# Weight sums of the up projections as a four-deep pipeline, and 16 instead of 8 blocks of layer 0 in seven products

## The chip, the cores and the metric

The kernel runs on one core of a Trainium2 chip. Its time is the device time of one launch, in microseconds (us). The core has TensorE (PE in the profile; PEld is its weight load), VectorE (DVE), ScalarE (ACT), GpSimd (POOL) and SyncE (SP). SP and POOL issue the large DMAs here: SP's go through the queue that the page calls q1 (hardware), POOL's through q0 (software). Both feed the same 16 DMA engines.

## The reference, cut to what matters

Two transformer layers over 512 tokens of width 1024, in fp32. Each is an attention and a feed-forward part:

```python
def conv_ffn(h, w_up, conv_w, conv_b, w_down):
    a, gate = jnp.split(h @ w_up, 2, axis=-1)          # w_up: 1024 x 5632
    a = lax.conv_general_dilated(a, ...) + conv_b      # 3 taps along the sequence
    return (jax.nn.silu(a) * gate) @ w_down            # w_down: 2816 x 1024

for i in range(2):
    x = x + attention_i(rms_norm(x, attn_norm[i]))     # layer 0: sliding window with sinks; layer 1: differential
    x = x + conv_ffn(rms_norm(x, ffn_norm[i]), ffn_w_up[i], ...)
return rms_norm(x, final_norm)
```

## The kernel before

**Products.** Every fp32 operand is cut into a high part (ACT writes it, rounded to fp32r) and a low part (DVE: the value less the high part). `hi_lo` (L764) makes one product of three matmuls (L766 to L768). The order on PE is written out by hand: attention of layer 0 (4 units), its output projection, 22 blocks of the up projection, 22 of the down projection, then the same for layer 1 with 8 units.

**The up projection, classical.** A block is 128 columns of `a` and the 128 matching columns of `gate`. `up_pair` (L1247) does two blocks. A block is 2 sides x 8 chunks of the contraction x 3 matmuls = 48 matmuls of 512 columns. Its weights are 1 MB, loaded by SP in two DMAs (L598).

**The up projection, in seven products.** `seven_products` (L1284) treats the block as a 2x2 block product (halves of the contraction, halves of the tokens, `a` against `gate`) and takes Strassen-Winograd's seven half-size products: 7 x 4 chunks x 3 = 84 matmuls of 256 columns. The left operands are weights and four sums of weights, S1 to S4. Per block SP loads 1.75 MB: in `load_seven` (L618) 0.25 MB (L629) and 0.5 MB (L630) of plain weights and 0.75 MB of sums (L631), in `load_fourth` (L605) 0.25 MB of S4 (L615). `PLAIN = (14, 6)` says how many blocks of each layer are classical: 14 of 22 in layer 0, 6 of 22 in layer 1. All load through the two halves of `raw`; a load waits until DVE has taken the low part of the block two before it, and ACT takes a block's high part once PE is done with the block two before it.

**The sums.** They lie in two DRAM tensors, `w_sums0` and `w_sums1`. POOL makes them with DMAs alone, in rounds (`weight_sums`, L727), each for 128 rows and 1024 columns: four copies DRAM to DRAM (L736 to L739), wait, two accumulating DMAs (L741, L742), wait, one (L744), wait, one (L746), wait. A DMA moves 0.5 MB. Layer 0 has one chunk of columns (`CHUNKS = (1, 2)`), so 4 rounds; layer 1 two chunks, so 8. SP waits (L625) for a chunk's sums ahead of the first load from it. `BEFORE_ROUND` holds POOL back: layer 0's round 0 until the load of attention unit 3 has landed, its round 3 until that of up block 3, and layer 1's round 2 until that of layer 1's unit 2. Rounds run without a stop otherwise.

## Time and profile before

| | us |
|---|---|
| median of 3 runs | 1111.3 (1111.16 to 1111.36) |
| the profiled execution | 1111.62 |
| its span in the profile | 1109.8 |
| rounds of sums of layer 0 begin at | 40.4, 73.2, 105.6, 178.0 |
| rounds of layer 1 begin at | 208.2, 250.0, 527.6, 569.7, 611.3, 652.7, 692.1, 731.3 |
| POOL's last DMA of layer 0 / of layer 1 is issued at | 202.7 / 765.3 |
| issue to landing of the second DMA of the up pairs issued at 194, 215, 226, 237, 259, 269 | 6.0, 8.5, 9.6, 7.0, 6.3, 6.5 |
| packets and MB, SP's queue / POOL's | 182430, 120.32 / 13824, 50.34 |
| SP issues the first load of a product block, layer 0 / layer 1 | 291.1 / 796.9 |

1.8 us of the profiled execution lie outside its span. "Idle before" in a timeline is the time that an engine stood still before an instruction, with what ended it. In a POOL row of a DMA the duration is that of issuing it only; when it landed is seen from the next row's wait. DMA share is the mean busy share of the 16 DMA engines in a stretch. PE's matmuls overlap one another, so the distance between two starts is what one costs, not its duration.

### The profile page before, as it was taken

How to read it: one execution, taken by the hardware profiler on the slowest of the kernel's cores; microseconds unless marked ns; L12 is line 12 of the kernel's file. 1: busy time of each engine (PE TensorE's matmuls, PEld its weight loads, DVE VectorE, ACT ScalarE, POOL GpSimd, SP SyncE). 2: the span in 40 equal slices, each digit the busy share in tenths (PEclk: the TensorE clock that was granted, in tenths of full speed). 3: DMA queues.
4: the chain of work that ended last, by engine and by line, in shares of the span. 5: the costliest groups of instructions: out<-in, count | busy, mean ns of one | idle time of the engine just before them, and what ended most of it. 6: DMA issues, size and time to landing. Idle time of an engine off the chain costs nothing.

```text
span 1109.8 us, 17573 instructions
## 1 busy us (share of the span) xinstructions
PE 1098.8 (99%) x6408; PEld 984.2 (89%) x6408; DVE 807.0 (73%) x1374; ACT 550.2 (50%) x1064; POOL 69.0 (6%) x116
## 2 busy tenths in 40 slices
PE   9999999999999999999999999999999999999997
PEld 8999888888899988888999999788889999998886
DVE  6888866557998863337788788857998888876335
ACT  6878653222255433335666666645344554443334
POOL 1111101111000000000111111110000000000000
PEclk9999999999999999999999999999999999999999
DMA  6767546999556422226888777777446656422322
GB/s 201 213 184 182 103 153 186 220 169 233 152 153 180 147 76 94 94 94 190 199 161 173 172 171 136 130 191 171 140 127 199 199 171 177 143 95 98 98 102 99
DMA packets 196330, 171.35 MB, mean 154 GB/s; under 512 B 14425, under 2 KB 176438, under 8 KB 196278
## 3 DMA queue, kind: packets, MB, share of 16 engines
q1 hardware_dynamic: 182430, 120.32, 35.9%
q0 software_dynamic: 13824, 50.34, 23.6%
q8 instruction: 31, 0.51, 0.2%
q14 instruction: 21, 0.17, 0.1%
q10 hardware_dynamic: 24, 0.01, 0.0%
HBM read 168.55 MB, written 52.43 MB: 199 GB/s over the span
## 4 chain that ended last, share of the span: by engine, by line
PE 91%; DVE 5%; ACT 2%; issue 1%; DMA 1%; SPq 0%; DVEq 0%; ACTq 0%
PE ps L766 23%; PE ps L767 23%; PE ps L768 23%; PE ps L842 15%; PE ps L883 2%; PE ps L1065 2%; PE ps L1084 1%; PE ps L944 1%; DMA raw<-in_a_w_in 1%; ACT w_hi L1429 1%; DVE w_lo L2012 0%; DVE h_lo L2044 0%; DVE xT L2376 0%; DVE x_tok L2731 0%; DVE ssacc L2037 0%
## 5 line engine op out<-in xcount | busy, mean ns | idle before, releaser
L768 PE MATMUL ps<-h_hi,w_hi 128*128 128x256 f32 (+1 forms) x704 | 233.2, 331 | 0.0
L767 PE MATMUL ps<-h_lo,w_hi 128*128 128x256 f32 (+1 forms) x704 | 233.2, 331 | 0.0
L766 PE MATMUL ps<-h_hi,w_lo 128*128 128x256 f32 (+1 forms) x704 | 233.2, 331 | 0.0
L1429 ACT ACTIVATE w_hi<-raw 128x512 fp32r<-128x512 f32 (+2 forms) x180 | 146.0, 842 | 86.0 <-PE ps L768 83.1
L2012 DVE TENSOR_TENSOR w_lo<-raw,w_hi 128x512 fp32r<-128x512 f32 (+2 forms) x180 | 167.9, 957 | 11.2 <-ACT w_hi L1429 11.0
L766 PEld LDWEIGHTS ps<-h_hi,w_lo 128*128 128x128 f32 x704 | 133.8, 190 | 12.6
L768 PEld LDWEIGHTS ps<-h_hi,w_hi 128*128 128x128 f32 x704 | 133.8, 190 | 12.5
L767 PEld LDWEIGHTS ps<-h_lo,w_hi 128*128 128x128 f32 x704 | 133.8, 190 | 12.4
L842 PE MATMUL ps<-w_hi,h_lo 128*128 128x384 f32 x368 | 126.1, 343 | 0.6 <-DVE w_lo L2012 0.4
L842 PE MATMUL ps<-w_hi,h_hi 128*128 128x384 f32 x368 | 125.7, 342 | 0.0
L842 PE MATMUL ps<-w_lo,h_hi 128*128 128x384 f32 x368 | 125.5, 341 | 0.0
L2405 DVE TENSOR_TENSOR u_lo<-u_all,u_hi 128x512 fp32r<-128x512 f32 x44 | 30.4, 691 | 123.4 <-ACT u_hi L1721 123.4
L1721 ACT ACTIVATE u_hi<-u_all 128x512 fp32r (+1 forms) x44 | 27.6, 631 | 142.2 <-PE ps L768 142.1
L766 PE MATMUL ps<-u_hi,w_lo 128*128 128x512 f32 (+1 forms) x272 | 95.9, 353 | 0.2
L768 PE MATMUL ps<-u_hi,w_hi 128*128 128x512 f32 (+1 forms) x272 | 95.6, 352 | 0.0
L767 PE MATMUL ps<-u_lo,w_hi 128*128 128x512 f32 (+1 forms) x272 | 95.6, 352 | 0.0
L2468 DVE TENSOR_TENSOR w_lo<-raw,w_hi 128x1536 fp32r<-128x1536 f32 x48 | 83.7, 1751 | 0.0
L842 PEld LDWEIGHTS ps<-w_hi,h_lo 128*128 128x128 f32 x368 | 69.2, 188 | 5.2 <-DVE v_lo L2067 2.9
L842 PEld LDWEIGHTS ps<-w_hi,h_hi 128*128 128x128 f32 x368 | 69.2, 188 | 0.8
L842 PEld LDWEIGHTS ps<-w_lo,h_hi 128*128 128x128 f32 x368 | 69.2, 188 | 0.3
L766 PE MATMUL ps<-w_hi,u_lo 128*128 128x512 f32 x176 | 68.6, 390 | 0.0
L768 PE MATMUL ps<-w_hi,u_hi 128*128 128x512 f32 x176 | 68.5, 389 | 0.0
(254 smaller groups left out, 2229.8 us busy)
## 6 DMA issues: line engine op xcount, KB each, us to landing
w_sums<-in_ffn_w_up POOLq DMA_DIRECT2D x72, 512.0 KB, 7.7
raw<-in_ffn_w_up SPq DMA_DIRECT2D x64, 512.0 KB, 5.2
raw<-in_ffn_w_down SPq DMA_DIRECT2D x44, 512.0 KB, 3.3
raw<-w_sums SPq DMA_DIRECT2D x24, 768.0 KB, 7.0
w_sums<-w_sums POOLq DMA_DIRECT2D x24, 512.0 KB, 7.3
raw<-in_b_w_in SPq DMA_DIRECT2D x24, 512.0 KB, 5.8
raw<-in_ffn_w_up SPq DMA_DIRECT2D x24, 256.0 KB, 3.0
s_raw<-w_sums SPq DMA_DIRECT2D x24, 256.0 KB, 3.7
```

The lines of the kernel that those rows point to most:

```text
L766: pe.matmul(out_, a_lo, b_hi, start=start, stop=False)
L767: pe.matmul(out_, a_hi, b_lo, start=False, stop=False)
L768: return pe.matmul(out_, a_hi, b_hi, start=False, stop=stop)
L842: ins = pe.matmul(ps[:, pj(u, t), 0:UW], a[:, kc, tok], b[:, kc, :], start=(kc == kc0 and m == 0), stop=(kc == kc1 and m == 2))
L883: ins = pe.transpose(ps[:, bank, c * P:(c + 1) * P], i, ident[:, :])
L944: ins = pe.matmul(ps[:, bank, 0:2 * P], head_queries(a)[:, g, :, :], keys_of(b, t, j), start=(m == 0), stop=(m == 2))
L1065: ins = pe.matmul(ps[:, s_bank(t) + e, 0:n], a[rows, 0, q], b[rows, 1, 0:n], start=(m == 0), stop=(m == 2))
L1429: act.activation(w_hi[:, s, at], raw[:, s, at], ACT.Copy).then_inc(hi_done, 1)
L1721: act.activation(u_hi[:, s, :], u_all[:, bass.ds(f, 1), :], ACT.Copy).then_inc(uhi_done, 1)
L2012: dve.tensor_tensor(w_lo[:, s, at], raw[:, s, at], w_hi[:, s, at].bitcast(F32), ALU.subtract).then_inc(lo_done, 1)
L2405: dve.tensor_tensor(u_lo[:, s, :], u_all[:, bass.ds(f, 1), :].rearrange("p a b -> p (a b)"), u_hi[:, s, :].bitcast(F32), ALU.subtract).the ...
L2468: dve.tensor_tensor(w_lo[:, s, at], raw[:, s, at], w_hi[:, s, at].bitcast(F32), ALU.subtract)\
```

## The change

`PLAIN` becomes `(6, 6)` and `CHUNKS` `(2, 2)`: layer 0 has 16 blocks in seven products too, and 8 rounds of sums in two chunks. Rounds are no longer done one after the other: step n issues the two additions of round n-1, the third addition of round n-2, the fourth of round n-3 and the four copies of round n, and then waits for all of them; a layer takes its rounds and three more steps. POOL is held back only at the beginning of each layer's sums: in layer 0 until the load of unit 2 (of attention) has landed, in layer 1 until that of its unit 2. `sums_in` is the new count for which SP waits: steps 0 to 6 for a layer's first chunk, all 11 for its second.

```diff
-PLAIN = (14, 6)
-CHUNKS = (1, 2)
+PLAIN = (6, 6)
+CHUNKS = (2, 2)
...
-BEFORE_ROUND = {(0, 0): ("attnA", 3), (0, 3): ("up0", 3), (1, 2): ("attnB", 2)}
+BEFORE_STEP = {(0, 0): ("attnA", 2), (1, 0): ("attnB", 2)}
...
             c = (f - PLAIN[l]) * P // SUM_COLS[l]
-            return ((CHUNKS[0] if l else 0) + c + 1) * HALF_D // P * DMAS * 16
+            steps = range(4 * c + 4 + 3)
+            n = 4 * CHUNKS[l]
+            before = 4 * CHUNKS[0] * DMAS if l else 0
+            return 16 * (before + sum(4 * (k < n) + 2 * (1 <= k <= n) + (2 <= k <= n + 1) + (3 <= k) for k in steps))
...
+                begun = 0
+                if n - 1 in range(len(rounds)):
+                    begun += add(block(n - 1, 0), part(n - 1, 0, F))
+                    begun += add(block(n - 1, 1), part(n - 1, 0, F))
+                if n - 2 in range(len(rounds)):
+                    begun += add(block(n - 2, 2), block(n - 2, 0))
+                if n - 3 in range(len(rounds)):
+                    begun += add(block(n - 3, 3), block(n - 3, 2))
+                if n in range(len(rounds)):
+                    begun += copy(block(n, 0), part(n, 1, F))
+                    begun += copy(block(n, 1), part(n, 0, 0))
+                    begun += copy(block(n, 2), part(n, 0, 0))
+                    begun += copy(block(n, 3), part(n, 1, 0))
+                return begun
...
-                for n, (c, rows) in enumerate(rounds):
-                    if (l, n) in BEFORE_ROUND:
-                        after_load(*BEFORE_ROUND[l, n])
-                    weight_sums(l, rows, c, done)
-                    done += DMAS * 16
+                for n in range(len(rounds) + 3):
+                    if (l, n) in BEFORE_STEP:
+                        after_load(*BEFORE_STEP[l, n])
+                    done += sum_step(l, n, rounds) * 16
+                    pool.wait_ge(sum_landed, done)
```

POOL's program before, one round of layer 0 and the beginning of the next. `w_sums0` is the DRAM tensor of layer 0's sums; L736 to L739 are copies, L741 to L746 additions:

```order
L736 DMA w_sums0<-in_ffn_w_up 128x1024 [waits sum_landed]
L737 DMA w_sums0<-in_ffn_w_up 128x1024
L738 DMA w_sums0<-in_ffn_w_up 128x1024
L739 DMA w_sums0<-in_ffn_w_up 128x1024
L741 DMA w_sums0<-in_ffn_w_up 128x1024 [waits sum_landed]
L742 DMA w_sums0<-in_ffn_w_up 128x1024
L744 DMA w_sums0<-w_sums0 128x1024 [waits sum_landed]
L746 DMA w_sums0<-w_sums0 128x1024 [waits sum_landed]
L736 DMA w_sums0<-in_ffn_w_up 128x1024 [waits sum_landed]
```

The same engine now, layer 0 from its step 3 to its step 5 (L745 is an addition, L750 a copy):

```order
L745 DMA w_sums0<-in_ffn_w_up 128x1024 [waits sum_landed]
L745 DMA w_sums0<-in_ffn_w_up 128x1024
L745 DMA w_sums0<-w_sums0 128x1024 x2
L750 DMA w_sums0<-in_ffn_w_up 128x1024 x4
L745 DMA w_sums0<-in_ffn_w_up 128x1024 [waits sum_landed]
L745 DMA w_sums0<-in_ffn_w_up 128x1024
L745 DMA w_sums0<-w_sums0 128x1024 x2
L750 DMA w_sums0<-in_ffn_w_up 128x1024 x4
L745 DMA w_sums0<-in_ffn_w_up 128x1024 [waits sum_landed]
```

Eight DMAs stood behind four waits; now eight stand behind one.

ACT's program before, in the feed-forward part of layer 0: a loop over two classical blocks (high parts of two blocks' weights, and two SiLUs), which runs four times, then the code that leads over to the product blocks. Before:

```order
L1806 UNCONDITIONAL_BRANCH
L1806 ISA
L1427 ISA
L1429 ACTIVATE w_hi<-raw 128x2048
L1725 ACTIVATE gated<-conv 128x512
L550 REGISTER_ALU
L1427 REGISTER_ALU
L1429 ACTIVATE w_hi<-raw 128x2048
L1725 ACTIVATE gated<-conv 128x512
L1806 REGISTER_ALU
L1806 COMPARE_AND_BRANCH
L1429 ACTIVATE w_hi<-raw 128x2048
```

Now the code that leads over stands at the head of the part:

```order
L1445 ACTIVATE w_hi<-raw 128x2048
L1741 ACTIVATE gated<-conv 128x512
L1445 ACTIVATE w_hi<-raw 128x2048
L1741 ACTIVATE gated<-conv 128x512
L1754 ACTIVATE u_hi<-u_all 128x1024
L1445 ACTIVATE w_hi<-raw 128x2048
L1741 ACTIVATE gated<-conv 128x512
L1754 ACTIVATE b21_ops<-u_all 128x1024
L1754 ACTIVATE b22_ops<-u_all 128x1024
L1445 ACTIVATE w_hi<-raw 128x2048
L1741 ACTIVATE gated<-conv 128x512
L1774 ACTIVATE w_hi<-raw 128x1536
```

The loop is gone (with 6 classical blocks it would run no time, as in layer 1), so the operands of the seven products are made from block 0 on instead of from block 8 on.

## Rows read from the trace of the kernel before

**Rows 1.** The page, part 1: busy us, share of the span, instructions, by engine.

```profile
PE 1098.8 (99%) x6408; PEld 984.2 (89%) x6408; DVE 807.0 (73%) x1374; ACT 550.2 (50%) x1064; POOL 69.0 (6%) x116
```

**Rows 2.** Timeline of PE at phase borders: start us, us, engine, line, operation.

```profile
152.69 0.39 PE L766 MATMUL ps<-ot_hi,w_lo 128*128 128x512 f32 x1
...
163.57 0.39 PE L766 MATMUL ps<-h_hi,w_lo 128*128 128x512 f32 x1
...
316.42 0.28 PE L766 MATMUL ps<-u_hi,w_lo 128*128 128x256 f32 x1
...
397.24 0.40 PE L766 MATMUL ps<-u_hi,w_lo 128*128 128x512 f32 x1
...
754.72 0.39 PE L766 MATMUL ps<-h_hi,w_lo 128*128 128x512 f32 x1
...
820.53 0.28 PE L766 MATMUL ps<-u_hi,w_lo 128*128 128x256 f32 x1
...
982.19 0.27 PE L1342 MATMUL ps<-ident,xT 128*128 128x128 f32 x1
```

**Rows 3.** Windows, product blocks: stretch, length, PE PEld DVE ACT POOL busy, clock, DMA, GB/s.

```profile
340.00:360.00 20.00, 20.00 (x169) 20.00 (x168) 16.86 (x23) 9.82 (x13) 0.00 (x0) 1.00 0.64 180
```

**Rows 4.** Timeline of POOL, two rounds of sums: last bracket is idle time before.

```profile
105.56 0.54 POOL L736 DMA_DIRECT2D w_sums<-in_ffn_w_up  x1 [4.56 <-DMA w_sums<-w_sums]
...
114.27 0.84 POOL L741 DMA_DIRECT2D w_sums<-in_ffn_w_up  x1 [6.61 <-DMA w_sums<-in_ffn_w_up]
...
122.64 0.81 POOL L744 DMA_DIRECT2D w_sums<-w_sums  x1 [6.67 <-DMA w_sums<-in_ffn_w_up]
...
128.18 0.80 POOL L746 DMA_DIRECT2D w_sums<-w_sums  x1 [4.73 <-DMA w_sums<-w_sums]
...
208.23 0.54 POOL L736 DMA_DIRECT2D w_sums<-in_ffn_w_up  x1 [4.76 <-DMA w_sums<-w_sums]
...
221.44 0.84 POOL L741 DMA_DIRECT2D w_sums<-in_ffn_w_up  x1 [11.06 <-DMA w_sums<-in_ffn_w_up]
...
233.03 0.81 POOL L744 DMA_DIRECT2D w_sums<-w_sums  x1 [9.89 <-DMA w_sums<-in_ffn_w_up]
...
250.02 0.54 POOL L736 DMA_DIRECT2D w_sums<-in_ffn_w_up  x1 [8.05 <-DMA w_sums<-w_sums]
```

**Rows 5.** One line's DMAs in a stretch (durations ns of the issue), then issue to landing.

```profile
L571 SPq DMA_DIRECT2D raw<-in_a_w_in x1: 5177/5177/5177, 24.4 to 24.4; - x1
DMA to landing us min/median/max: 9.4/9.4/9.4
...
L592 SPq DMA_DIRECT2D raw<-in_a_w_out x1: 368/368/368, 142.6 to 142.6; - x1
DMA to landing us min/median/max: 4.7/4.7/4.7
...
L598 SPq DMA_DIRECT2D raw<-in_ffn_w_up x2: 373/408/442, 776.6 to 777.2; - x2
DMA to landing us min/median/max: 3.8/4.2/4.7
...
L598 SPq DMA_DIRECT2D raw<-in_ffn_w_up x2: 373/842/1312, 225.9 to 226.4; - x2
DMA to landing us min/median/max: 8.4/9.0/9.6
...
L631 SPq DMA_DIRECT2D raw<-w_sums x1: 436/436/436, 356.6 to 356.6; - x1
DMA to landing us min/median/max: 7.1/7.1/7.1
```

**Rows 6.** Timelines of ACT, DVE and PE around block 20 of layer 0.

```profile
367.74 1.47 ACT L1758 ACTIVATE w_hi<-raw 128x1536 fp32r<-128x1536 f32 x1
...
373.60 1.75 DVE L2468 TENSOR_TENSOR w_lo<-raw,w_hi 128x1536 fp32r<-128x1536 f32 x1
...
377.08 0.28 PE L766 MATMUL ps<-u_hi,w_lo 128*128 128x256 f32 x1
```

More of the change, by code:

```diff
@@ L725, in _ @@
                     pool.memset(tensor[(1 - e) * HD:(2 - e) * HD, e, :].bitcast(F32), 0.0).then_inc(kz_done, 1)
-            def weight_sums(l, rows, c, done):
-                wv, sums = ffn_w_up[l], w_sums[l]
-                a, gate = PLAIN[l] * P + c, PLAIN[l] * P + c + F
-                def part(half, at):
-                    return wv[half * HALF_D + rows:half * HALF_D + rows + P, at:at + SUM_COLS[l]]
-                s1, s3, s2, s4 = (sums[q * HALF_D + rows:q * HALF_D + rows + P, c:c + SUM_COLS[l]] for q in range(4))
-                pool.dma_start(s1, part(1, gate)).then_inc(sum_landed, 16)
-                pool.dma_start(s3, part(0, a)).then_inc(sum_landed, 16)
-                pool.dma_start(s2, part(0, a)).then_inc(sum_landed, 16)
-                pool.dma_start(s4, part(1, a)).then_inc(sum_landed, 16)
-                pool.wait_ge(sum_landed, done + 4 * 16)
-                pool.dma_start(s1, part(0, gate), accum_op=ALU.add, max_dma_last_dim=4 * SUM_COLS[l]).then_inc(sum_landed, 16)
-                pool.dma_start(s3, part(0, gate), accum_op=ALU.add, max_dma_last_dim=4 * SUM_COLS[l]).then_inc(sum_landed, 16)
-                pool.wait_ge(sum_landed, done + 6 * 16)
-                pool.dma_start(s2, s1, accum_op=ALU.add, max_dma_last_dim=4 * SUM_COLS[l]).then_inc(sum_landed, 16)
-                pool.wait_ge(sum_landed, done + 7 * 16)
-                pool.dma_start(s4, s2, accum_op=ALU.add, max_dma_last_dim=4 * SUM_COLS[l]).then_inc(sum_landed, 16)
-                pool.wait_ge(sum_landed, done + 8 * 16)
@@ L749, in after_load, with sum_step, part, block @@
             def after_load(ph, i):
                 pool.wait_ge(raw_landed[i % 2], landed(ph, i % 2, i // 2))
+            def sum_step(l, n, rounds):
+                def part(r, half, at):
+                    c, rows = rounds[r]
+                    at += PLAIN[l] * P + c
+                    return ffn_w_up[l][half * HALF_D + rows:half * HALF_D + rows + P, at:at + SUM_COLS[l]]
+                def block(r, q):
+                    c, rows = rounds[r]
+                    return w_sums[l][q * HALF_D + rows:q * HALF_D + rows + P, c:c + SUM_COLS[l]]
+                def add(to, what):
+                    pool.dma_start(to, what, accum_op=ALU.add, max_dma_last_dim=4 * SUM_COLS[l])\
+                        .then_inc(sum_landed, 16)
+                    return 1
+                def copy(to, what):
+                    pool.dma_start(to, what).then_inc(sum_landed, 16)
+                    return 1
+                begun = 0
[12 more added lines that the diff above has]
+                return begun
```

## The prediction

> **What bounds the kernel now.** First the page's busy line: PE is busy 99% of the span [rows 1], so a change pays only through what PE has to do, or costs by making PE stand still. Then the timeline of PE at the borders of the phases, since busy time tells nothing of the distance between matmuls. In layer 0 the 14 classical blocks take from 163.57 to 316.42, 152.85 us, 10.92 each (0.45 of it are two extra matmuls in all); the 8 product blocks take from 316.42 to 397.24, 80.82 us, 10.10 each [rows 2]. So seven products save 7.5% of a block, not an eighth: 84 matmuls come 0.120 apart, 48 come 0.227 apart. Third, POOL and the DMA queues, which cost nothing now because PE does not wait for them: what matters is how much room they have.
>
> **Term 1, PE's work.** Eight blocks go over: 8 x (10.92 - 10.10) = 6.5 us less. Layer 1, which has 6 and 16 blocks already, is the check, since layer 0 will have its code: 754.72 to 982.19 is 227.47 us, against 233.67 for layer 0's 163.57 to 397.24 [rows 2]. The difference is 6.2 us, with the making of the operands in it, which in layer 1 lies in blocks 0 to 5 and costs PE nothing visible (its six classical blocks end at 820.53, after 65.81 us, 10.97 each [rows 2]). I take 6.2. The loop that disappears from ACT and the earlier operand work are in that figure.
>
> **Term 2, when layer 0's first chunk of sums is ready.** SP wants it for block 6. Blocks keep their distance up to there, so that load, issued for block 14 at 291.1, comes 87 us (eight classical blocks) earlier, at 204.
>
> What one DMA costs POOL's queue: in a round with no load beside it the four copies take 105.56 to 114.27, 8.7 us; two additions to 122.64, 8.4; one to 128.18, 5.5 [rows 4]. So a wait has a fixed part of about 2.3 us, an addition moves for about 3.1 and four copies for 6.4. A step of eight is 4 x 3.1 + 6.4 + 2.3 = 21 us, where a round took 28 (its fourth addition counted like the third). Steps 0 to 6 are 8.7, 15, 18 and four times 21, in all 126 us. They begin when unit 2's load has landed, 24.4 + 9.4 = 33.8 [rows 5], not at 40.4. SP's loads share the engines meanwhile: three of 1.5 MB, one of 1 MB and five pairs of 1 MB, 10.5 MB. A round with some 3.5 MB of loads beside it took 208.23 to 250.02, 41.8 us [rows 4], which is 4 us per MB; that is the upper end, and 1 us per MB (loads that fall into the waits) the lower. I take 3.2, nearer to the upper, since the pipeline leaves few waits to hide in: 34 us. Sum: 33.8 + 126 + 34 = 194; bounds 170 and 205. So the chunk is just ready at 204, and the second one, four steps later, long before block 14. The price of the wait itself is nothing at 194 and near nothing at 205.
>
> **Term 3, what is left of the sums beside the product blocks' loads.** This is new: before, POOL's queue was empty from about 288 (the second round of layer 1) and again from about 773, both ahead of the first product load of a layer. Now four steps (8, 4, 2 and 1 DMAs) come after 194: 21 + 14.7 + 8.5 + 5.5 = 50 us with nothing beside them, of which 10 are done by 204. 40 are left: 31 moving, 9 fixed.
>
> A product block needs 1.75 MB per 10.1 us. In the stretch of product blocks the DMA engines are at a share of 0.64 with no sums [rows 3]: 6.4 us of every 10.1. How SP's queue fares beside POOL's: a pair of 1 MB alone takes 776.6 to 777.2 + 4.7, so 5.2 us, some 2.9 of it moving; beside two additions it takes from 225.9 to 226.4 + 9.6, so 10.2 us, 7.9 moving [rows 5]. SP's queue gets 2.9/7.9 = 0.37 of the engines there, while the additions stretch from 8.4 to 11.6 us (221.44 to 233.03 [rows 4]) and keep about 0.63. Beside copies and single additions SP got more; 0.6 is my other bound. Eleven of the fifteen DMAs left are additions, so I take 0.43, near the first.
>
> At 0.43 the sums need 31/0.57 + 9 = 63 us. In these SP's queue does 54 x 0.43 + 9 = 32 us of work, 5.0 blocks of 6.4, while PE wants 63/10.1 = 6.2: it is 1.2 blocks, 12 us, behind. Against that stands the room: the load for block 20 lands at 356.6 + 7.1 = 363.7 [rows 5] and ACT takes it up at 367.74; DVE finishes at 373.60 + 1.75 = 375.35 and PE begins the block at 377.08 [rows 6]. That is 4.0 + 1.7 = 5.7 us. So PE stands still for 12 - 5.7 = 6.5 us, in blocks 8 to 11. Behind a late load ACT's in-order program holds the SiLU, the first tap and the copy out of PSUM of the block before, on which DVE waits, so a late load isn't forgiven elsewhere. At 0.37: 31/0.63 + 9 = 58 us, 4.2 blocks done of 5.7, 15 behind, 9.5 lost. At 0.5: 71 us, 6.3 of 7.0, 7 behind, 1 lost. At 0.6: nothing.
>
> The Trainium skill, DMA: Bandwidth & Descriptors, Queues, rings and completion order, says that an engine round-robins between queues at packet granularity. Read as strict alternation that speaks against this change: with the packets of the table (some 660 bytes each on SP's queue, 3640 on POOL's) an estimate by the rule is that SP gets 0.15 of the bytes, a product load takes over 40 us, and the time would be past 1130. The trace disagrees (10.2 us for 1 MB beside additions [rows 5]), and the sum goes by the trace.
>
> **Term 4, smaller places.** The last load of the output projection (1 MB) is issued at 142.6 and lands after 4.7 us [rows 5] with POOL at rest, which it no longer is. PE wants it at 152.69 [rows 2]; its first quarter has to pass ACT and DVE, a third of a 1.47 and of a 1.75 us conversion [rows 6], 1.1 us. So it may take 8.9 us. Beside copies or additions 4.7 becomes 8 to 10.5: 0 to 1.6 us, and the same in layer 1. I take 1.3 for both. Layer 1's sums start at 527 and take 50 us per four steps as here; the first chunk is ready around 720, the second near 800, where the first product load is issued at 796.9: 0 to 1 us, I take 0. Before, all of layer 1's attention ran beside sums with PE at work, so I leave it at nothing.
>
> **The sum.** -6.2 + 6.5 + 1.3 = +1.6, on the profiled execution's 1111.62 (a span of 1109.8 and 1.8 around it): 1113.2. That execution is 0.3 above the median, so 1112.9 on the median. This is the likeliest case: the gain on PE is real and is given back as stalls behind loads.
>
> **Rivals.**
> A. *The loads keep up.* SP's queue gets 0.5 or more beside the sums, or the sums are through earlier (at 170 instead of 194 only 16 us of them are left at 204, and the room covers that). For it: in the table the pairs at 194, 259 and 269 landed 6 to 6.5 us after their issue beside sums; against it: those at 215 and 226. 1111.3 - 6.2 = 1105.1, up to 1108.5 with part of the stalls.
> B. *The sums come late as well.* If steps are not shorter than rounds when the queue is full (28 instead of 21 us for each of the four full steps), the first chunk is ready at 222. The load for block 6 then lands near 236, where ACT would have taken it at 218.6 (305.7 less 87): some 12 us lost after the room, and term 3 on top at its full 9.5. 1111.3 - 6.2 + 12 + 9.5 = 1126.6; with the first chunk at 206 and a share of 0.37 it is some 1117 to 1120. It decides from a first chunk later than about 208.
> C. *The change doesn't do what it says, in part*: the pipeline shortens nothing, since the engines and not the waits bound a round. That is the first half of B.
> D. *Only the attention parts lose*: term 3 is nothing, but the output projections and layer 1's units (1.5 MB every 24 us, beside a queue that is always full) lose 3 to 5 us. 1108 to 1110.
>
> **Numbers.** Forecast (stalls of 4 to 10 us in all, 1109.3 to 1115.5) 0.42; A 0.37; B with C 0.15; D 0.06. The predicted time is 1112.9. A measurement of this kernel can tell 0.2% (2.2 us) from no change. A is faster (0.37), of D half; of the forecast 0.24 is within 0.2% and 0.18 slower; B slower. So faster 0.40, same 0.27, slower 0.33. The range goes from A's lower end, 1104.8, to the milder half of B, 1119; about 0.15 is left out.
>
> **What would show it.** PE's borders: the up projection of layer 0 in 227.5 us and no idle PE would be A. For the forecast PE must show idle time ahead of L782 to L784 in blocks 8 to 11 (235 to 285 us), put down to DVE's low weights, with ACT's L1774 waiting for a DMA; SP's product loads there must take over 11 us to land instead of 7.1, and the same loads after POOL's last DMA of layer 0 (expected near 265) about 7. Step lengths on POOL near 21 us without loads confirm term 2, near 27 C. I am wrong if the product loads land in under 10 us while POOL's queue is full, or if the sums of layer 0 are through before 230.

## The result, and the profile after

| | us |
|---|---|
| median of 4 runs | 1146.4 (1144.32 to 1146.85) |
| the profiled execution / its span | 1146.85 / 1145.1 |
| ratio to the kernel before | 1.031, 95% interval 1.030 to 1.033 |
| forecast | 1112.9, range 1104.8 to 1119.0 |

The changed kernel is 35 us slower, and the forecast missed both the time and its range. The L numbers of PE, ACT and DVE named here are 16 higher than before (L766 to L768 are L782 to L784, L1758 is L1774), those of SP's loads 3 higher (L598 is L601, L631 is L634).

The page of the changed kernel, part 1 (answers [rows 1]) and the timeline of PE at the phase borders ([rows 2]):

```profile
PE 1102.8 (96%) x6696; PEld 999.9 (87%) x6696; DVE 824.6 (72%) x1406; ACT 568.6 (50%) x1096; POOL 90.6 (8%) x148
```

```profile
163.31 0.39 PE L782 MATMUL ps<-h_hi,w_lo 128*128 128x512 f32 x1
...
265.99 0.58 PE L782 MATMUL ps<-u_hi,w_lo 128*128 128x256 f32 x1 [6.75 <-DVE w_lo L2484]
...
431.24 0.40 PE L782 MATMUL ps<-u_hi,w_lo 128*128 128x512 f32 x1
...
789.98 0.39 PE L782 MATMUL ps<-h_hi,w_lo 128*128 128x512 f32 x1
...
855.79 0.28 PE L782 MATMUL ps<-u_hi,w_lo 128*128 128x256 f32 x1
...
1017.45 0.38 PE L1358 MATMUL ps<-ident,xT 128*128 128x128 f32 x2
```

Layer 0's up projection takes 431.24 - 163.31 = 267.9 us, where layer 1's, with the same code, takes 227.5 as before. So 40.5 us are lost there. Six classical blocks, 65.8 us in layer 1, take 102.7 (+36.9); the 16 product blocks take 165.25 (+3.6 against layer 1's 161.66). From 431.24 to 789.98 it is 1.3 us more than before. Take away 6.2 us of work and 0.3 us by which the up projection begins earlier, and the 35.3 us are left by which the spans differ.

Where PE stood still in these blocks (timeline of PE; the bracket is the idle time and what ended it). The number after the start is the duration of one matmul; 0.39 is the usual one for 512 columns:

```profile
187.52 0.76 PE L820 MATMUL ps<-ss_lo,ones_r 128*128 128x512 f32 x1 [13.18 <-DVE ss_lo L2416]
...
217.49 0.79 PE L782 MATMUL ps<-h_hi,w_lo 128*128 128x512 f32 x1 [4.76 <-DVE w_lo L2028]
...
245.16 0.80 PE L782 MATMUL ps<-h_hi,w_lo 128*128 128x512 f32 x1 [4.17 <-DVE w_lo L2028]
```

With the 6.75 us at 265.99 these are 28.9 us. Counted from start to start, with a fifth of 1.3 us at 278.6, it is 31. The rest of the 40.5, some 9.5, is clock. Windows of the changed kernel (stretch, length, busy time of PE, PEld, DVE, ACT, POOL, granted clock, DMA share, GB/s):

```profile
174.00:187.00 13.00, 0.35 (x2) 0.00 (x0) 3.21 (x3) 2.54 (x2) 5.44 (x8) 0.72 1.01 240
187.00:195.00 8.00, 7.48 (x21) 5.94 (x22) 4.86 (x8) 5.03 (x5) 0.00 (x0) 0.61 0.98 116
195.00:212.00 17.00, 17.00 (x77) 14.07 (x76) 7.92 (x10) 0.00 (x0) 1.39 (x3) 1.00 1.00 248
...
266.00:276.00 10.00, 10.00 (x62) 10.00 (x63) 8.55 (x11) 2.95 (x4) 0.81 (x1) 0.71 1.01 209
...
380.00:400.00 20.00, 20.00 (x169) 20.00 (x168) 17.02 (x22) 9.98 (x12) 0.00 (x0) 1.00 0.63 184
```

After each of these stalls PE went on at half its rate for a while (0.76 to 0.80 us a matmul instead of 0.39 is the lower of the two levels, 1.2 GHz). So the window from 187 to 195 has a granted clock of 0.61 though PE is busy, which costs some 3 us (8 x 0.39), and the one from 266 to 276 another 3 (10 x 0.29). The last line answers [rows 3]: product blocks with no sums beside them are as before.

Who made PE wait. The chain behind the first stall, timelines of SP, ACT and DVE, and under SP's row the landing of the same pair of DMAs (weights of up block 1):

```profile
153.79 0.99 SPq L601 DMA_DIRECT2D raw<-in_ffn_w_up  x2
...
DMA to landing us min/median/max: 24.6/25.7/26.9
...
181.16 1.91 ACT L1445 ACTIVATE w_hi<-raw 128x2048 fp32r<-128x2048 f32 x1 [12.85 <-DMA raw<-in_ffn_w_up]
186.02 0.63 ACT L1729 ACTIVATE ss_hi<-ssacc 128x512 fp32r<-128x512 f32 x1 [2.96 <-DVE ssacc L2053]
...
183.10 2.29 DVE L2028 TENSOR_TENSOR w_lo<-raw,w_hi 128x2048 fp32r<-128x2048 f32 x1 [14.20 <-ACT w_hi L1445]
```

The pair landed at 153.79 + 24.6 and 154.2 + 26.9 = 181.1; a pair alone takes 3.8 and 4.7 [rows 5]. ACT, which works in order, stood before L1445 for 12.85 us, and DVE stood for 14.20 us before its low part of the same weights (L2028). The last addition of the squares (L2053), the mean square of the input (L1729, then PE's L820) stood behind the two, though they need no weights at all. ACT's waits over the whole run (us in all, times, longest):

```profile
ACT w_hi L1445 <- DMA raw<-in_ffn_w_up: 42.9, 3, 18.2
ACT w_hi L1774 <- DMA raw<-w_sums: 23.7, 2, 16.3
```

POOL's steps, first DMA of each (answers [rows 4]; the bracket is the wait for the step before):

```profile
47.89 1.72 POOL L745 DMA_DIRECT2D w_sums<-in_ffn_w_up  x2 [11.06 <-DMA w_sums<-in_ffn_w_up]
69.89 1.68 POOL L745 DMA_DIRECT2D w_sums<-in_ffn_w_up  x2 [18.20 <-DMA w_sums<-in_ffn_w_up]
95.63 1.70 POOL L745 DMA_DIRECT2D w_sums<-in_ffn_w_up  x2 [21.14 <-DMA w_sums<-in_ffn_w_up]
120.77 1.70 POOL L745 DMA_DIRECT2D w_sums<-in_ffn_w_up  x2 [19.52 <-DMA w_sums<-in_ffn_w_up]
147.05 1.70 POOL L745 DMA_DIRECT2D w_sums<-in_ffn_w_up  x2 [20.84 <-DMA w_sums<-in_ffn_w_up]
179.67 1.69 POOL L745 DMA_DIRECT2D w_sums<-in_ffn_w_up  x2 [27.17 <-DMA w_sums<-in_ffn_w_up]
210.61 1.70 POOL L745 DMA_DIRECT2D w_sums<-in_ffn_w_up  x2 [25.50 <-DMA w_sums<-in_ffn_w_up]
```

The steps last 13.3 (from 34.58), 22.0, 25.7, 25.1, 26.3, 32.6 and 30.9 us. The first chunk is ready at 210.6; the last DMA of layer 0 is issued at 272.8. The late chunk itself held nobody up: SP issued its first load of a product block at 228.9, and what it had waited for was DVE's low part of earlier, late weights (SP's waits from 205 to 232; us in all, times, longest):

```profile
SPq L632 <- DVE w_lo L2028: 9.0, 1, 9.0
```

The queues in 30 us of the long step that began at 147 (packets, MB, share of the 16 engines' time):

```profile
q0 software_dynamic: 1141, 4.16, 78.4%
q1 hardware_dynamic: 3740, 1.92, 24.5%
```

SP gets a quarter of the engines: 1.9 MB in 30 us, where classical blocks want 1 MB per 10.9.

### The profile page after: what moved, and what is told of

The parts are those of the page before. It is cut to its first block, busy times and chain, and to the rows that moved or that the text cites. A ratio compares the mean times of both kernels' runs of the same rounds, so it can differ in the third digit from the quotient of the medians.

```text
span 1145.1 us, 18313 instructions
## 1 busy us (share of the span) xinstructions
PE 1102.8 (96%) x6696; PEld 999.9 (87%) x6696; DVE 824.6 (72%) x1406; ACT 568.6 (50%) x1096; POOL 90.6 (8%) x148
## 3 DMA queue, kind: packets, MB, share of 16 engines
q0 software_dynamic: 18432, 67.12, 31.2%
## 4 chain that ended last, share of the span: by engine, by line
PE 77%; DMA 12%; DVE 7%; ACT 2%; SPq 1%; issue 1%; DVEq 0%; ACTq 0%
PE ps L782 20%; PE ps L784 19%; PE ps L783 19%; PE ps L858 13%; DMA raw<-in_ffn_w_up 6%; DMA raw<-in_b_w_out 3%; PE ps L899 2%; DMA raw<-w_sums 2%; DVE w_lo L2028 1%; PE ps L1081 1%; PE ps L1100 1%; ACT w_hi L1445 1%; PE ps L960 1%; SPq L632 1%; DMA raw<-in_a_w_out 1%
## 5 line engine op out<-in xcount | busy, mean ns | idle before, releaser
L782 PE MATMUL ps<-h_hi,w_lo 128*128 128x256 f32 (+1 forms) x704 | 223.3, 317 | 8.9 <-DVE w_lo L2028 8.9
L783 PE MATMUL ps<-h_lo,w_hi 128*128 128x256 f32 (+1 forms) x704 | 222.8, 316 | 0.0
L784 PE MATMUL ps<-h_hi,w_hi 128*128 128x256 f32 (+1 forms) x704 | 222.4, 316 | 0.0
L2028 DVE TENSOR_TENSOR w_lo<-raw,w_hi 128x512 fp32r<-128x512 f32 (+2 forms) x172 | 149.6, 896 | 24.9 <-ACT w_hi L1445 24.8
L1445 ACT ACTIVATE w_hi<-raw 128x512 fp32r<-128x512 f32 (+2 forms) x172 | 130.6, 792 | 63.6 <-DMA raw<-in_ffn_w_up 42.9
L782 PEld LDWEIGHTS ps<-h_hi,w_lo 128*128 128x128 f32 x704 | 136.6, 194 | 18.0 <-DVE w_lo L2028 9.8
L784 PEld LDWEIGHTS ps<-h_hi,w_hi 128*128 128x128 f32 x704 | 136.5, 194 | 8.2
L782 PE MATMUL ps<-u_hi,w_lo 128*128 128x512 f32 (+1 forms) x304 | 105.7, 348 | 8.1 <-DVE w_lo L2484 7.8
L2484 DVE TENSOR_TENSOR w_lo<-raw,w_hi 128x1536 fp32r<-128x1536 f32 x64 | 111.8, 1752 | 0.0
L783 PE MATMUL ps<-u_lo,w_hi 128*128 128x512 f32 (+1 forms) x304 | 105.2, 346 | 0.0
L784 PE MATMUL ps<-u_hi,w_hi 128*128 128x512 f32 (+1 forms) x304 | 105.2, 346 | 0.0
L750 POOL DMA_DIRECT2D w_sums<-in_ffn_w_up x64 | 49.1, 1487 | 336.6 <-DMA raw<-in_b_w_in 288.3
L782 PEld LDWEIGHTS ps<-u_hi,w_lo 128*128 128x128 f32 x304 | 58.1, 191 | 16.2 <-DVE w_lo L2484 8.8
```

The lines of the kernel that those rows point to most:

```text
L750: pool.dma_start(to, what).then_inc(sum_landed, 16)
L782: pe.matmul(out_, a_lo, b_hi, start=start, stop=False)
L783: pe.matmul(out_, a_hi, b_lo, start=False, stop=False)
L784: return pe.matmul(out_, a_hi, b_hi, start=False, stop=stop)
L1445: act.activation(w_hi[:, s, at], raw[:, s, at], ACT.Copy).then_inc(hi_done, 1)
L2028: dve.tensor_tensor(w_lo[:, s, at], raw[:, s, at], w_hi[:, s, at].bitcast(F32), ALU.subtract).then_inc(lo_done, 1)
```

## Experiments

Two questions stood at the start: do the sums cost the time at all, and is it that the pipeline keeps POOL's queue full, that SP gets few turns beside long packets, or that there is twice as much to sum? Medians in us; "before" in the sessions was 1111.2 to 1111.3. Each is 4 runs or more; "ratio" is the 95% interval of the ratio to the kernel before.

| run | what differs | median | ratio |
|---|---|---|---|
| no_sums | changed kernel, no sums | 1104.7 | 0.993 to 0.996 |
| pipe_14_6 | pipeline, old split | 1111.6 | 1.000 to 1.002 |
| serial_6_6 | new split, old rounds | 1177.5 | 1.057 to 1.065 |
| small_packets | changed, 512-byte packets | 1159.3 | 1.042 to 1.046 |
| after_contig | changed, rows of sums 4 KB apart | 1123.9 | 1.010 to 1.014 |
| pipe_14_6_wide | pipe_14_6, rows 8 KB apart | 1116.7 | 1.003 to 1.006 |
| before_contig | before, layer 1's rows 4 KB apart | 1111.1 | 0.999 to 1.001 |
| contig_hold | after_contig, POOL held twice more | 1113.2 | 1.001 to 1.003 |
| contig_half | after_contig, four DMAs at a time | 1107.1 | 0.994 to 0.998 |
| after_half | changed, four at a time, 8 KB apart | 1159.7 | 1.040 to 1.048 |
| pad_4608 | after_contig, 4.5 KB apart | 1121.2 | 1.006 to 1.010 |
| pad_8704 | changed, 8.5 KB apart | 1122.0 | 1.008 to 1.011 |

**no_sums.** POOL issues nothing, SP doesn't wait for sums and loads as many bytes of plain weights in their place, so the product blocks multiply other numbers. Of the edit:

```diff
...
-                if is_block(f, PLAIN[l], PLAIN[l] + SUM_COLS[l] // P):
-                    sp.wait_ge(sum_landed, sums_in(l, f))
...
-                for n in range(len(rounds) + 3):
+                for n in range(0):
```

> The changed kernel without any weight sums: POOL makes none, SP does not wait for them and loads plain weights of the same size in their place (the 12 chunks and the 4 of the fourth sum), so the seven products are made from other operands. It measures term 1 alone. Both theories (turns: SP's small packets wait behind POOL's large ones; volume: too many bytes in all) expect no stall: layer 0's up projection 227.5 us, the kernel near 1105. More than 1107 would say that something else than the sums costs time.

1104.7 us: 6.4 less than before in the same session, 41.7 less than the changed kernel, and no stall on PE in the up projection. So term 1 (6.2) holds, and all of the loss is the sums' doing.

**pipe_14_6.** The pipeline alone.

```diff
-PLAIN = (6, 6)
-CHUNKS = (2, 2)
+PLAIN = (14, 6)
+CHUNKS = (1, 2)
```

> The pipeline alone: 14 classical blocks in layer 0 and its four rounds in one chunk, as before, in pipelined steps without a hold. POOL's queue is full from 34 to about 180 and the bytes are those of before. Turns: the load of up block 1, issued near 154, lands late all the same, PE waits for the mean square some 5 to 13 us, and the kernel takes 1116 to 1130. Volume: there are no more bytes than before, so within 3 us of 1111.

1111.6, as before. POOL's timeline:

```profile
46.04 1.72 POOL L745 DMA_DIRECT2D w_sums<-in_ffn_w_up  x2 [8.98 <-DMA w_sums<-in_ffn_w_up]
59.78 1.68 POOL L745 DMA_DIRECT2D w_sums<-in_ffn_w_up  x2 [9.95 <-DMA w_sums<-in_ffn_w_up]
78.35 1.80 POOL L745 DMA_DIRECT2D w_sums<-in_ffn_w_up  x2 [13.98 <-DMA w_sums<-in_ffn_w_up]
101.43 1.70 POOL L745 DMA_DIRECT2D w_sums<-in_ffn_w_up  x2 [17.54 <-DMA w_sums<-in_ffn_w_up]
```

The queue was empty by 128, before the up blocks' loads began (at 142.8), so this run could say nothing on sums beside them. But it showed what no theory had: the first steps are the same DMAs beside the same loads as in the changed kernel, and took 11.2, 13.7, 18.6 and 23.1 us instead of 13.3, 22.0, 25.7 and 25.1.

**serial_6_6.** The old rounds, one after the other, with the new split (the `PLAIN` and `CHUNKS` of the change in the kernel before, POOL held only at each layer's beginning).

```diff
-PLAIN = (14, 6)
-CHUNKS = (1, 2)
-BEFORE_ROUND = {(0, 0): ("attnA", 3), (0, 3): ("up0", 3), (1, 2): ("attnB", 2)}
+PLAIN = (6, 6)
+CHUNKS = (2, 2)
+BEFORE_ROUND = {(0, 0): ("attnA", 2), (1, 0): ("attnB", 2)}
```

> The 16 product blocks alone: the rounds of before, one after the other with four waits each, 8 for layer 0 in two chunks, begun after unit 2's load. Turns: the classical zone shows little stall (under 5 us) since POOL's queue drains four times a round; but 8 rounds of 33 to 42 us end near 330 and the second chunk is wanted near 285, so about 40 us are lost there at block 14: 1140 to 1150. Volume: stalls in the classical zone as large as in the changed kernel (30 us), and the second chunk's wait on top, 1160 or more.

1177.5. A round took 40.0, 37.1, 38.3 and 39.7 us, against 32.8 and 32.4 for the first two in the kernel before, in nearly the same stretch; the second chunk came late (SP waited 48.6 us for it), and PE stood still for 33.4 us up to 362.9. So the pipeline isn't to blame for slow sums: both kinds are slower with the new split. But in the classical blocks PE stood still for only 3.5 us, where the changed kernel loses 22: rounds, with at most four DMAs under way, hold SP's loads up less than steps of eight. "Turns" had that part right, and the time wrong.

**small_packets.** POOL's packets as small as SP's, for turns by packet.

```diff
-                    pool.dma_start(to, what, accum_op=ALU.add, max_dma_last_dim=4 * SUM_COLS[l])\
+                    pool.dma_start(to, what, accum_op=ALU.add, max_dma_last_dim=512)\
...
-                    pool.dma_start(to, what).then_inc(sum_landed, 16)
+                    pool.dma_start(to, what, max_dma_last_dim=512).then_inc(sum_landed, 16)
```

> The changed kernel with POOL's DMAs, copies and additions, cut into runs of 512 bytes instead of 4096. Turns: SP's loads get an equal turn; the pair for block 1 lands in under 12 us instead of 25 and the stall before the mean square is gone; the sums take longer, so the first chunk may come late. 1115 to 1140, with its loss at another place. Volume: loads land as late as in the changed kernel or later, 1147 or more.

1159.3. From the third on, steps grew to 31 to 39 us with four times the packets, the first chunk came at 244.6, and PE stood 14.2 us before the first product block. As "turns" expected, up block 1's pair landed in 4.3 and 11.5 us and the stall before the mean square was gone; but that pair was issued at 162.2, when five of POOL's eight DMAs had landed and its last three were just being issued. Of the loads amid a full group, up block 3's pair took 14.3 and 25.6 us (23.2 and 25.8 in the changed kernel), and SP's queue had 29.3% of the engines from 175 to 208, against 24.5% above. So shorter packets give SP little, if anything, and make POOL's DMAs dearer; the run doesn't show that the packets' size has no part in it.

**A new theory.** What differs between pipe_14_6 and the changed kernel in those first steps is the tensor that the sums are written to. With 8 blocks in seven products `w_sums0` has 1024 columns, its rows are 4 KB apart; with 16 it has 2048, and rows are 8 KB apart. Layer 1's was that wide already. Three runs test it, and two more its rivals.

**after_contig.** One tensor per chunk, both layers; the loads index the chunk's tensor.

```diff
-        w_sums = [nc.dram_tensor(f"w_sums{l}", (4 * HALF_D, (FB - PLAIN[l]) * P), F32) for l in range(2)]
+        w_sums = [[nc.dram_tensor(f"w_sums{l}_{c}", (4 * HALF_D, SUM_COLS[l]), F32) for c in range(CHUNKS[l])]
+                  for l in range(2)]
...
-                    return w_sums[l][q * HALF_D + rows:q * HALF_D + rows + P, c:c + SUM_COLS[l]]
+                    return w_sums[l][c // SUM_COLS[l]][q * HALF_D + rows:q * HALF_D + rows + P, :]
```

> The changed kernel with one DRAM tensor of 1024 columns per chunk of sums, for both layers, instead of one of 2048: a row of sums lies 4 KB from the next instead of 8 KB, as layer 0's did before the change. Same DMAs, same bytes, same order, same waits. Pitch theory (the sums are slow because their rows lie 8 KB apart): steps of eight in layer 0 fall from 22 to 27 us to 14 to 20 us, the first chunk is ready before 175 us instead of at 210.6, the loads of the up blocks land in under 10 us, and the time is 1105 to 1113. Load theory (a queue of eight DMAs at a time and SP's loads share the engines, whatever the rows' distance): steps stay within 2 us of the changed kernel's, and the time stays 1140 to 1150.

1123.9, that is 22.5 us less than the changed kernel, with the same DMAs and bytes. POOL:

```profile
45.52 1.72 POOL L746 DMA_DIRECT2D w_sums<-in_ffn_w_up  x2 [9.01 <-DMA w_sums<-in_ffn_w_up]
59.18 1.68 POOL L746 DMA_DIRECT2D w_sums<-in_ffn_w_up  x2 [9.87 <-DMA w_sums<-in_ffn_w_up]
...
158.97 1.70 POOL L746 DMA_DIRECT2D w_sums<-in_ffn_w_up  x2 [15.66 <-DMA w_sums<-in_ffn_w_up]
```

The first chunk is ready at 159 instead of 210.6. On the page, POOL's queue takes less of the engines for the same 18432 packets and 67 MB. The changed kernel's line, then this one's:

```profile
q0 software_dynamic: 18432, 67.12, 31.2%
```

```profile
q0 software_dynamic: 18432, 67.12, 23.5%
```

But neither expectation met the time: the steps did nearly as the theory of distance says (18 to 23 us for the full ones, 14 to 20 expected), the loads didn't (below).

**pipe_14_6_wide.** The other way round: in pipe_14_6, the narrow tensor made 2048 columns wide, half of it unused.

```diff
-        w_sums = [nc.dram_tensor(f"w_sums{l}", (4 * HALF_D, (FB - PLAIN[l]) * P), F32) for l in range(2)]
+        w_sums = [nc.dram_tensor(f"w_sums{l}", (4 * HALF_D, 2048), F32) for l in range(2)]
```

> The pipeline with layer 0's old split (14 classical blocks, one chunk, four rounds), but layer 0's sums in a tensor of 2048 columns of which only 1024 are used: rows 8 KB apart instead of 4 KB, everything else as in the run with the pipeline alone (whose steps were 11.2, 13.7, 18.6, 23.1, 13.1, 8.5 us). Pitch theory: steps of 13, 22, 26, 26 us and more, as in the changed kernel; the queue still empties before 170, so PE loses little: 1111 to 1114. Load theory: steps as without the padding, within 1 us each, and 1111.6.

```profile
48.75 1.72 POOL L745 DMA_DIRECT2D w_sums<-in_ffn_w_up  x2 [10.41 <-DMA w_sums<-in_ffn_w_up]
70.59 1.68 POOL L745 DMA_DIRECT2D w_sums<-in_ffn_w_up  x2 [18.05 <-DMA w_sums<-in_ffn_w_up]
96.13 1.70 POOL L745 DMA_DIRECT2D w_sums<-in_ffn_w_up  x2 [20.95 <-DMA w_sums<-in_ffn_w_up]
```

Steps of 12.7, 21.8, 25.5 and 25.6 us, those of the changed kernel, with nothing changed but unused columns; 1116.7 us, 5 more than without the padding. The excess over the expectation is one 3.8 us stall up to 156.4, behind the output projection's last load, which took 12.4 us beside a queue that was now busy until 160, and the lower clock after it (0.65 from 156.4 to 165).

**before_contig.** Layer 1's tensor of the kernel before split in the same way.

> The kernel before with layer 1's sums in two tensors of 1024 columns, one per chunk, instead of one of 2048; layer 0's are as they were. Pitch theory: layer 1's rounds fall from 41.8 us (208 to 250) and 42 to 39 us (from 527 on) to 28 to 33 us as in layer 0; the time stays 1110 to 1112, since POOL's queue holds nobody up. Load theory (the 41.8 us came from loads beside them): rounds stay near 40 us, and the time the same.

Rounds in layer 1 fell from 39 to 42 us to 31 to 35 us (527.1, 561.1, 592.6, 623.4, 658.1 and 689.3 are their starts), and the one that took 41.8 us in [rows 4] to 32.8 (206.9 to 239.7). The start of a round's copies and of its additions, for one round of layer 1 in the kernel before and for one here:

```profile
569.71 0.54 POOL L736 DMA_DIRECT2D w_sums<-in_ffn_w_up  x1 [6.78 <-DMA w_sums<-w_sums]
582.71 0.84 POOL L741 DMA_DIRECT2D w_sums<-in_ffn_w_up  x1 [10.81 <-DMA w_sums<-in_ffn_w_up]
```

```profile
592.63 0.54 POOL L737 DMA_DIRECT2D w_sums<-in_ffn_w_up  x1 [4.57 <-DMA w_sums<-w_sums]
602.32 0.84 POOL L742 DMA_DIRECT2D w_sums<-in_ffn_w_up  x1 [7.60 <-DMA w_sums<-in_ffn_w_up]
```

Four copies take 13.0 us with rows 8 KB apart and 9.7 with 4 KB in these two rounds, 11.4 to 13.0 and 8.6 to 11.5 in all. The time is the same, since no one waited for POOL. So most of what the 41.8-us round had over a 28-us one (9 of 13.8 us) was the tensor's, not the loads'.

**pad_4608, pad_8704.** Is it that 128 rows of 4 KB are one unbroken piece of memory, the distance as such, or its being 8 KB exactly? 128 unused columns for the tensors of after_contig (pad_4608) and for those of the changed kernel (pad_8704, shown):

```diff
-        w_sums = [nc.dram_tensor(f"w_sums{l}", (4 * HALF_D, (FB - PLAIN[l]) * P), F32) for l in range(2)]
+        w_sums = [nc.dram_tensor(f"w_sums{l}", (4 * HALF_D, (FB - PLAIN[l] + 1) * P), F32) for l in range(2)]
```

> As the run with one tensor per chunk (1123.9 us, steps 11.2, 13.7, 18.2, 22.9, 18.6, 19.0, 21.1 us), with 128 unused columns per row: rows 4.5 KB apart, a DMA's 128 rows no longer one unbroken piece of memory. If sums are fast there because a DMA writes an unbroken piece, steps grow to 13, 22, 26, 25 us as in the changed kernel and the time to 1140 and more. If it is the distance of 8 KB (or its being such a round number) that makes them slow, steps stay within 1 us of the unpadded ones and the time within 4 us of 1123.9.

> The changed kernel with 128 unused columns in its one tensor of sums per layer: rows 8.5 KB apart instead of 8 KB, everything else as it was. If it is the round 8 KB that slows the sums (rows falling on the same part of the memory again and again), steps fall from 13, 22, 26, 25, 26, 33 us to 11 to 23 us as with rows 4 KB apart and the time to 1120 to 1128. If it is that a DMA's rows are not one unbroken piece, or the distance as such, steps and time stay: 1140 to 1150.

1121.2 and 1122.0. In pad_8704 steps begin at

```profile
45.91 1.72 POOL L745 DMA_DIRECT2D w_sums<-in_ffn_w_up  x2 [9.18 <-DMA w_sums<-in_ffn_w_up]
60.57 1.69 POOL L745 DMA_DIRECT2D w_sums<-in_ffn_w_up  x2 [10.87 <-DMA w_sums<-in_ffn_w_up]
78.36 1.85 POOL L745 DMA_DIRECT2D w_sums<-in_ffn_w_up  x2 [13.20 <-DMA w_sums<-in_ffn_w_up]
```

that is 11.4, 14.7 and 17.8 us each; in pad_4608 the first seven are 10.6, 14.2, 19.5, 23.2, 19.4, 18.5 and 22.4 us, within 1.3 of after_contig's. Neither the unbroken piece nor the larger distance matters; of the four distances tried, 8 KB alone is slow. A change of one expression takes 24 us off the changed kernel.

**What is left above 1104.7.** With the distance mended, PE still stood still in after_contig, for 8.2 us up to 160.5 and for 5.2 up to 189.7:

```profile
160.48 0.77 PE L783 MATMUL ps<-ot_hi,w_lo 128*128 128x512 f32 x1 [8.18 <-DVE w_lo L2029]
...
189.68 0.77 PE L821 MATMUL ps<-ss_lo,ones_r 128*128 128x512 f32 x1 [5.15 <-DVE ss_lo L2417]
```

Look at when SP's loads land. The output projection's last load, issued at 142.06, took 16.8 us: it landed at 158.9, and POOL's step of eight, begun at 137.87, was through at 158.97. In the changed kernel the pair for up block 1 landed at 178.4 and 181.1, POOL's step at 179.67; the pair issued at 185.6 landed its first half at 208.7, POOL's step was through at 210.6. In these rows an SP load issued in the middle of a group of POOL's DMAs lands about when the group is through. If so, what counts is how long a group is, and two runs try that.

**contig_hold.** POOL waits for up block 1's load ahead of step 6 and for block 3's ahead of step 7.

```diff
-BEFORE_STEP = {(0, 0): ("attnA", 2), (1, 0): ("attnB", 2)}
+BEFORE_STEP = {(0, 0): ("attnA", 2), (0, 6): ("up0", 1), (0, 7): ("up0", 3), (1, 0): ("attnB", 2)}
```

> The changed kernel with one tensor per chunk of sums (rows 4 KB apart), and POOL held in layer 0 at two more places: step 6 until the load of up block 1 has landed (about 150 us instead of 137.9), step 7 until that of up block 3 has (about 175 to 180 instead of 159). With the tensors alone, 1123.9 us, PE stood still 8.3 us at 151.9 behind the output projection's last load (16.8 us to land) and 5.3 us at 184.1 behind up block 1's (19.8 us). Contention theory (what is left above 1105 are SP's loads in the shadow of steps of eight DMAs): both gaps go, at most 2 us of idle PE is left, and the time is 1105 to 1110; layer 0's sums end near 235 instead of 218, and the second chunk is still in time at 287. Otherwise (the loads are slow for a reason of their own): the loads take 15 us and more as well, and the time stays above 1118.

1113.2, 10.7 less than after_contig. Both stalls went (the last output load lands after 4.8 us), and new ones of 1.2 and 4.5 us came, up to 186.6 and 213.1, since the loads issued at 160.4 and 186.7, in the middle of the steps that had moved there, took 19.0 and 18.6 us. The holds moved the shadow to where it cost less; they didn't shorten it.

**contig_half.** Groups of at most four DMAs.

```diff
                 if n in range(len(rounds)):
+                    if begun:
+                        pool.wait_ge(sum_landed, done + begun * 16)
                     begun += copy(block(n, 0), part(n, 1, F))
```

> The same kernel with one tensor per chunk, no further holds, but a wait between the additions and the copies of each step, so that at most four of POOL's DMAs are under way instead of eight. If SP's loads are slow because POOL's queue is never empty (turns by queue), a second pause of some 2 us per step changes little: output projection's last load 12 to 16 us, time 1116 to 1124. If they are slow because eight DMAs stand in the engines at once (a load waits behind what is in them), loads fall to 8 to 10 us, and the time to 1106 to 1112. Steps grow by 2 to 4 us in both, the first chunk is ready near 175.

1107.1, 0.4% less than the kernel before. The page, and POOL around the output projection's end:

```profile
PE 1091.6 (99%) x6696; PEld 991.7 (90%) x6696; DVE 824.3 (75%) x1406; ACT 569.6 (52%) x1096; POOL 90.6 (8%) x148
```

```profile
132.44 1.70 POOL L746 DMA_DIRECT2D w_sums<-in_ffn_w_up  x2 [6.81 <-DMA w_sums<-in_ffn_w_up]
...
146.44 2.08 POOL L751 DMA_DIRECT2D w_sums<-in_ffn_w_up  x4 [10.64 <-DMA w_sums<-w_sums]
157.26 1.70 POOL L746 DMA_DIRECT2D w_sums<-in_ffn_w_up  x2 [8.74 <-DMA w_sums<-in_ffn_w_up]
```

The output projection's last load landed 6.9 us after 142.3, at 149.3, 2.8 behind the group that was through at 146.44, and up block 1's pair after 5.7 and 7.2. Others still end with their group: the load issued at 143.4 landed at 157.2 (group through at 157.26), that at 161.7 at 173.1 (172.55), that of S4 at 207.6 at 226.2 (226.68). But a group now lasts 9 to 18 us, and that is nearly within the room that PE has. The first chunk is ready at 183.6 instead of 159.0, which no one minds. In layer 0's up projection PE stands still for 1.6 us in all, where it was 30 in the changed kernel.

The queues over 30 us of each kernel while SP loads up blocks: in the changed one SP's had 24.5% (above); here, from 142 to 172,

```profile
q0 software_dynamic: 1326, 4.78, 62.6%
q1 hardware_dynamic: 6225, 3.67, 41.5%
```

SP moves 3.67 MB in that time instead of 1.92, and POOL 4.78 instead of 4.16. Part of that is the distance, part the pauses.

**after_half.** The same wait in the changed kernel as it is, rows 8 KB apart.

> The changed kernel as it is (sums in one tensor of 2048 columns per layer, rows 8 KB apart) with only the further wait between the additions and the copies of each step. It completes a square: with rows 4 KB apart the further wait took the time from 1123.9 to 1107.1. If the two causes are separate (depth of POOL's queue, distance of the rows), the loads of the up blocks land in 6 to 14 us as there, but two-part steps take 25 to 31 us, the first chunk is ready at 215 to 230 instead of 210.6, and SP's product loads come late: 1120 to 1140, between. If the rows' distance alone makes the loads slow, nothing is won: 1143 to 1155. If the depth alone does, 1106 to 1112.

1159.7, worse by 13 and outside all three expectations. In the classical blocks the wait did its work here too: PE stood still for 5.6 us in five places, instead of 22 in the changed kernel, and up block 1's pair landed after 8.1 and 9.3 us (block 2's, amid the next group, after 18.0 and 19.7). But steps last 28 to 36 us from the third on, and the first chunk is ready at 229.5, within the bounds; SP, now earlier at that place, waited 24.2 us for it. The price of that was set too low:

```profile
259.46 0.58 PE L784 MATMUL ps<-u_hi,w_lo 128*128 128x256 f32 x1 [21.76 <-DVE w_lo L2486]
```

PE stood 21.8 us before the first product block and 14 more in the next ones, beside the second chunk's steps. So the further wait is worth 16.8 us with rows 4 KB apart and costs 13.3 with 8 KB: it shortens the groups at the price of later sums, and with slow sums the chunk has no room for that.

## Why the prediction was wrong, point by point

**Bound and term 1** held: 6.2 us less work was forecast, and 6.4 were measured with the sums taken out.

**Term 2** failed. The price of a step, 21 us, was put together from a round of layer 0 [rows 4], which wrote to a tensor with rows 4 KB apart; the change doubles that tensor's width. Loads included, steps 0 to 6 were to take 126 + 34 = 160 us and took 176 (34.6 to 210.6). The difference between layer 0's 28-us round and layer 1's 41.8 was laid on SP's loads, as 3.2 us per MB (at its own upper price of 4 us per MB the bound is 202, not 205). The table of rounds already spoke against that: layer 0's last round, begun at 178.0 beside three pairs of loads, took 30.3 us, and the next, layer 1's first, beside about as many, 41.8. before_contig shows that the tensor is most of it. The two errors leaned against each other (a price without the tensor's part, and loads that carried it), so the chunk was forecast for 194 and came at 210.6, outside the bounds of 170 to 205. With rows 4 KB apart the same steps end at 159, after 125 us: step and loads together were priced too high there. The path was wrong as well. Term 2 asked only whether the chunk comes too late for block 6, and it did not hold SP up (the row of SP's wait above); slow sums cost time because each group of eight took longer, and with it every load beside it.

**Term 3** is the step that failed most, in size and in place. Its share of 0.43 started from 0.37, from the pair that landed 10.2 us after 225.9 [rows 5]. But POOL's two additions were through at 232.8, and the pair landed behind them, at 234.2 and 236.0; the share was taken over a stretch that the end of POOL's group had cut short. Beside a full group of eight SP had 0.245 of the engines (POOL 0.78). And I looked for the shortage only in the product blocks, from 204 on, since only their loads are larger. The classical blocks were hit first and harder, with 36.9 us of the 40.5: with 1.9 MB in 30 us SP can't feed 1 MB per 10.9. The mechanism, PE standing behind late loads, was right, at 31 us instead of 6.5.

The Trainium skill, DMA: Bandwidth & Descriptors, Queues, rings and completion order, has the engines alternate between queues at packet granularity. By it I had given an estimate of over 40 us per product load and a time past 1130, and written that the trace disagrees. The trace of before disagreed for pairs beside two DMAs; with eight under way the worst product load took 22.1 us, and SP had 0.32 of the bytes (1.92 of 6.08 MB), twice the estimate's 0.15. small_packets, with four times as many and shorter packets on POOL's queue, raised SP's share of the engines' time from 24.5% to 29.3% only, so the rule isn't confirmed as read. The estimate also took the profile's packets for those of the Trainium skill, which are groups of descriptors. That the time came out past 1130 is luck for the estimate: its product loads of over 40 us were not seen, and most of the loss lay in the classical blocks.

**A term was missing**: after each stall PE went on at the lower clock for some us (granted clocks of 0.61 and 0.71 in the windows above), in all some 9.5 us of the 40.5.

**Term 4** (1.3) was put on both output projections. Layer 0's last output load took 6.9 us and cost nothing. The stretch from 431.24 to 789.98 is 1.3 us longer, but 1.0 of it is a wait up to 714.35 in layer 1's attention (PE's L899 for DVE's qk), and PE's waits in layer 1's output projection are those of before (0.4 and 0.2): the size agrees by luck.

**The rivals.** B (steps no shorter than rounds, chunk at 222, 1126.6) was the nearest: four of the seven steps took 25 to 31 us, one 32.6, the chunk came at 210.6. But it priced the late chunk itself, which cost nothing, so its nearness is in part luck; after_half and serial_6_6 are the runs in which a late chunk costs. Its reason, that the engines and not the waits bound a round, is not what the runs show: pipe_14_6 has layer 0's four rounds in 93 us (34.8 to 128) instead of four times 28 to 33, so the pipeline does what it says, and with the tensor mended the first chunk is ready at 159. B had no cause for longer steps and no price for classical blocks, so its 15% and the range were too small. A (1105.1) is what contig_half nearly reaches, at 1107.1.

**The signs** given in the prediction: idle PE in blocks 8 to 11, put down to DVE's low weights, was not seen; the last wait was 1.3 us at 278.6, before block 7, and the others lay in blocks 0 to 6. Product loads over 11 us: yes (22.1, 17.8), and about 7 after POOL's last DMA. Steps near 21: no. POOL's last DMA of layer 0 near 265: 272.8.

**The sum of the result.** 1104.7 with no sums; 19.2 more for the sums with rows 4 KB apart, eight DMAs at a time (after_contig), of which four at a time give back 16.8; 22.5 more for rows 8 KB apart: 1146.4. The two aren't independent, as after_half shows.

## What to carry to other kernels

When a change makes an array larger or gives it another shape, look at what its row distance becomes before taking over prices measured with the old one; where that is 8 KB (no other round number was tried here), try a few hundred bytes of padding first, since it is one expression. Work in the background on a shared set of DMA engines is to be cut into groups no longer than the slack of the foreground's loads: in these runs a load issued amid a group landed about when the group was through, so the group's length tells more than the share of bytes. But look at what the cutting does to the end of the background work (after_half). A share or a rate is to be read over a stretch in which both sides have work to the end.

## What the runs showed of the hardware that was not expected

DRAM to DRAM copies and additions of 128 rows of 4 KB are slower when the rows lie exactly 8 KB apart than with 4, 4.5 or 8.5 KB: layer 0's steps 3 to 5 took 25.1, 26.3 and 32.6 us with 8 KB and 22.9, 18.6 and 19.0 with 4 KB, a round's four copies in layer 1 11.4 to 13.0 us instead of 8.6 to 11.5, and the packets of POOL's queue took 36% more of the engines' time for the same bytes (31.2% of 1145 us against 23.5% of 1121). The Trainium skill, DMA: Bandwidth & Descriptors, Latency and other measured facts, has a row on HBM row pitch at large powers of two, with losses from 2 MiB on, for other tiles, where 4 KiB of padding restored the rate and 192 bytes did not. Here a loss shows at 8 KB, with additions among the DMAs, and 512 bytes of padding take it away (1146.4 to 1122.0); whether it is the same effect isn't shown. Why is open: whether it is the write, the read of the sum in an accumulating DMA, or two rows falling on the same part of the memory wasn't tried apart. That copies alone got slower says that it isn't the accumulation alone.

A load issued on SP's queue amid a group of POOL's DMAs landed about when the group was through, not after a time of its own: after 16.8, 19.0 and 24.6 us beside groups of eight, where such a load alone took 3.8 to 4.7. SP's queue also stood in its issues: the issue at 161.62 in the changed kernel took 13.6 us instead of 0.4, so the loads behind it started late as well. With no sums the longest issue of the whole run took 5.3 us.
